# A block step with attention and 16,384 experts: the products of the first 96 expert tiles taken as one of 512 columns and one of 256, and the halves of a bank added afterwards

## What is computed

```
q = (h @ w_q).reshape(C, PEER_HEADS, 2, D_KEY // 2)
s = jnp.einsum('cphd,phkd->cphk', q, sub_keys)
s1, i1 = lax.top_k(s[:, :, 0], PEER_TOPK); s2, i2 = lax.top_k(s[:, :, 1], PEER_TOPK)
cand = s1[..., :, None] + s2[..., None, :]; cidx = i1 * N_KEYS + i2   # all pairs
top_s, top_i = lax.top_k(cand, PEER_TOPK);  e = cidx at top_i;  g = softmax(top_s)
a = jax.nn.gelu(jnp.einsum('cpkd,cd->cpk', u_tab[e], h))
f = jnp.einsum('cpk,cpkd->cd', g * a, v_tab[e])
```

## Time and profile before

| | |
|---|---|
| median of 3 runs | 1099.77 us (1098.5 to 1102.85) |
| the profiled execution | 1107.55 us, of which its span is 1105.9 us |
| busy share of the span | PE 96%, PEld 86%, DVE 77%, ACT 50%, POOL 12% |
| 512 KB loads and 128 KB stores of the up tiles | 128 each |

### The profile page before, as it was taken

The page is one execution under the profiler, slowest core; times in us unless marked ns, Lnnn a source line. Parts: engine busy times, 40 slices in busy tenths (PEclk is TensorE's granted clock), DMA queues, the critical chain, the costliest instruction groups (busy, mean ns, idle before and its releaser), DMA issues.

```text
span 1105.9 us, 23553 instructions
## 1 busy us (share of the span) xinstructions
PE 1066.5 (96%) x7256; PEld 954.3 (86%) x7256; DVE 856.9 (77%) x1950; ACT 555.2 (50%) x1057; POOL 137.8 (12%) x153
## 2 busy tenths in 40 slices
PE   6999989889999999999999999999999999999996
PEld 6997645879999999999999999998788888888875
DVE  4324353788988888887658999978888888888877
ACT  4435454544453544443554555545555555555543
POOL 0244401100001000454100000001010101010100
PEclk9999986989999999999999999999999999999998
DMA  7655903243458866899974444458888888888872
GB/s 252 259 204 185 350 39 115 84 145 115 139 186 276 272 236 230 310 409 392 319 249 140 139 140 143 142 165 276 319 284 296 281 294 286 296 286 289 293 236 90
DMA packets 96248, 253.19 MB, mean 229 GB/s; under 512 B 11424, under 2 KB 44224, under 8 KB 95408
## 3 DMA queue, kind: packets, MB, share of 16 engines
q1 hardware_dynamic: 81840, 196.84, 51.5%
q0 software_dynamic: 14368, 55.87, 14.4%
HBM read 232.60 MB, written 22.12 MB: 230 GB/s over the span
## 4 chain that ended last, share of the span: by engine, by line
PE 85%; DMA 7%; DVE 4%; ACT 2%; issue 1%; SPq 0%; DVEq 0%; ACTq 0%
PE ps L541 13%; PE ps L542 13%; PE ps L543 12%; PE ps L993 10%; PE ps L995 10%; PE ps L994 10%; DMA activations<-u_out 6%; PE ps L966 5%; PE ps L625 1%; DVE w_lo L1358 1%; PE ps L897 1%; PE ps L772 1%; DMA a_in<-activations 1%; PE ps L980 1%; PE ps L769 0%
## 5 line engine op out<-in xcount | busy, mean ns | idle before, releaser
L1358 DVE TENSOR_TENSOR w_lo<-ring,w_hi 128x512 fp32r<-128x512 f32 (+1 forms) x458 | 389.5, 853 | 137.7 <-ACT w_hi L1041 124.1
L1041 ACT CAST w_hi<-ring 128x512 fp32r<-128x512 f32 (+1 forms) x460 | 345.8, 752 | 98.7 <-PE ps L995 62.5
L541 PE MATMUL ps<-h_hi,w_hi 128*128 128x256 f32 (+1 forms) x1128 | 330.6, 293 | 3.0 <-DVE w_lo L1358 3.0
L542 PE MATMUL ps<-h_lo,w_hi 128*128 128x256 f32 (+1 forms) x1128 | 321.0, 285 | 0.0
L543 PE MATMUL ps<-h_hi,w_lo 128*128 128x256 f32 (+1 forms) x1128 | 319.3, 283 | 0.0
L541 PEld LDWEIGHTS ps<-h_hi,w_hi 128*128 128x128 f32 x1128 | 214.9, 191 | 7.0 <-issue 3.9
L542 PEld LDWEIGHTS ps<-h_lo,w_hi 128*128 128x128 f32 x1128 | 214.2, 190 | 0.0
L543 PEld LDWEIGHTS ps<-h_hi,w_lo 128*128 128x128 f32 x1128 | 211.8, 188 | 0.0
L993 PE MATMUL ps<-w_hi,y_hi 128*128 128x512 f32 x512 | 199.8, 390 | 0.7 <-DVE y_lo L1823 0.5
L994 PE MATMUL ps<-w_hi,y_lo 128*128 128x512 f32 x512 | 199.2, 389 | 0.0
L995 PE MATMUL ps<-w_lo,y_hi 128*128 128x512 f32 x512 | 199.2, 389 | 0.0
(11 more groups left out here) (349 smaller groups left out, 1274.9 us busy)
## 6 DMA issues: line engine op xcount, KB each, us to landing
ring<-in_uT_dram SPq DMA_DIRECT2D x128, 512.0 KB, 3.6
ring<-in_v_dram SPq DMA_DIRECT2D x128, 512.0 KB, 4.4
activations<-u_out SPq DMA_DIRECT2D x128, 128.0 KB, 3.3
a_in<-activations SPq DMA_DIRECT2D x128, 128.0 KB, 4.2
ring<-in_w_in_dram SPq DMA_DIRECT2D x22, 512.0 KB, 4.4
ring<-in_w_q_dram SPq DMA_DIRECT2D x16, 512.0 KB, 3.2
ks<-in_cache_sb_dram POOLq DMA_DIRECT2D x16, 256.0 KB, 3.2
vs<-in_cache_sb_dram POOLq DMA_DIRECT2D x16, 256.0 KB, 5.4
```

What stands on the lines that cost most here:

```text
L541: mm(out, hi, hi_, start=start, stop=False)
L542: mm(out, hi, lo_, start=False, stop=False)
L1041: nc.scalar.copy(w_hi[slot][:, x], ring[:, ring_slot, x]).then_inc(part_hi, 2 if half is None else 1)
L1358: V.tensor_tensor(w_lo[slot][:, x], ring[:, ring_slot, x], w_hi[slot][:, x].bitcast(F32), ALU.subtract).then_inc(part_lo[ring_slot], 2 if ...
```

## The change

The two copies of `h` are placed as one tile `h_both` with a fixed distance between the low and the high half, so that one matmul can stream 256 low columns and 256 high columns. For the first 96 up tiles, `up_tile` issues for each block of rows one product of `w_hi` with 512 columns (low half of the bank: `w_hi*h_lo`; high half: `w_hi*h_hi`) and one of `w_lo` with `h_hi`, 256 columns, into the high half: 16 matmuls instead of 24. The two halves must then be added. ACT copies the low half to `u_sum` (four buffers), DVE adds the high half to it (`halves_added`), and ACT takes gelu from there.

The order on ACT changes with it: `up_step` of tile t issues `high` of tile t + 4 first, then the copy of tile t, then gelu of tile t - 1. DVE adds the halves of tile t directly behind `low` of tile t + 4. PE waits for the addition of tile t - 4 before it writes that bank again. `PACE` goes from 1.2 to 1.05. `u_sum` lies where `w_lo` of the gate stage's second slot lies, so DVE waits for gelu of the last tiles before it goes on to the gates. SP's program, the 32 up tiles of the gate stage, and the down tiles are not changed.

```diff
-PACE, PACE_Q = 1.2, 2.0
+PACE, PACE_Q = 1.05, 2.0
...
+        h_apart = at_h - (at_con + NLIVE)
+        h_both = at("h_both", [128, 2, h_apart], at_con + NLIVE, F32R)
...
+        u_sum = at("u_sum", [128, 4, DT], at_w1 + 3 * D)
...
+            def up_tile(slot, bank, lows):
+                both = ps[:, bank, :].rearrange("p (a t) -> p a t", a=2)
+                for kd in range(KD):
+                    if kd % 4 == 0:
+                        pe.wait_ge(lows[0], lows[1 + kd // 4])
+                    block_ = slice(kd * 128, (kd + 1) * 128)
+                    last = kd == KD - 1
+                    if last:
+                        mm(both[:, 1, :], w_lo[slot][:, block_], h_hi[:, kd, 0:DT], start=False, stop=False)
+                    ins = mm(both, w_hi[slot][:, block_], h_both[:, :, kd * T:kd * T + DT], start=kd == 0, stop=last)
+                    if not last:
+                        ins = mm(both[:, 1, :], w_lo[slot][:, block_], h_hi[:, kd, 0:DT], start=False, stop=False)
+                    if kd % 4 == 3:
+                        ins.then_inc(w_mm, 1)
...
-                        pe.wait_ge(u_act, 4 * i + r + 1)
-                        project((AT_U + r) % 4, h_parts, r, halves(i, AT_U + r), width=DT)
+                        pe.wait_ge(u_add, 4 * i + r + 1)
+                        up_tile((AT_U + r) % 4, r, halves(i, AT_U + r))
...
-            def gelu_then_high(i, r, first=0):
-
-                gelu(i, r, first)
-                n = AT_U + first + r + 4
-                slot, value = filled(n)
-                high(slot, 16 * i + value, place(n))
+                t = first + r
+                if first < U_ALONE:
+                    act.wait_ge(u_add, 4 * i + (4 + t + 1))
+                else:
+                    act.wait_ge(w_mm, 8 * i + 2 * (AT_U + t + 1))
+                if t >= 2:
+                    act.wait_ge(spill[t % 2], 32 * i + 16 * (t // 2))
+                x = u_sum[:, t % 4, :] if first < U_ALONE else ps[:, r, 0:DT]
+                A(u_out[:, t % 2, :], x, ACT.Gelu_apprx_tanh).then_inc(u_act, 1)
+
+            def up_step(i, r, first=0, next_high=True):
+
+                n = AT_U + first + r
+                if next_high:
+                    slot, value = filled(n + 4)
+                    high(slot, 16 * i + value, place(n + 4), used=8 * i + 2 * (n + 1))
+                else:
+                    act.wait_ge(w_mm, 8 * i + 2 * (n + 1))
+                nc.scalar.copy(u_sum[:, r % 4, :], ps[:, r % 4, 0:DT]).then_inc(u_low, 1)
+                if first + r >= 1:
+                    gelu(i, r - 1, first)
...
+            def halves_added(m):
+                dve.wait_ge(u_low, m + 1)
+                V.tensor_tensor(u_sum[:, m % 4, :], u_sum[:, m % 4, :], ps[:, m % 4, DT:2 * DT], ALU.add).then_inc(u_add, 1)
...
                 lows[0] = n + 1
+                if n >= AT_U + 4:
+                    halves_added(n - AT_U - 4)
...
+            halves_added(U_ALONE - 4)
             low_half(0, m0, 0)
             low_half(0, m0, 1)
+            halves_added(U_ALONE - 3)
+            dve.wait_ge(u_act, 4 + U_ALONE - 2)
             low_half(0, m0 + 1, 0)
+            halves_added(U_ALONE - 2)
+            halves_added(U_ALONE - 1)
+            dve.wait_ge(u_act, 4 + U_ALONE)
```

More of the change, by code:

```diff
@@ L246, in trunk @@
         os_ = at("os_", [128, 2, 128], at_w1 + 1536)
-        h_hi = at("h_hi", [128, KD, T], at_h, F32R)
-        h_lo = at("h_lo", [128, KD, T], at_con + NLIVE, F32R)
+        h_apart = at_h - (at_con + NLIVE)
+        h_both = at("h_both", [128, 2, h_apart], at_con + NLIVE, F32R)
+        h_lo, h_hi = [h_both[:, q, 0:KD * T].rearrange("p (c t) -> p c t", t=T) for q in range(2)]
         E = [at_e + 2 * D * q for q in range(4)]
@@ L349, in trunk @@
         rt_exp_in, rt_exp, rt_pick, rt_t, rt_slot = map(sem, ("rt_exp_in", "rt_exp", "rt_pick", "rt_t", "rt_slot"))
-        u_act, one_ready, g_mm, g_sb = map(sem, ("u_act", "one_ready", "g_mm", "g_sb"))
+        u_act, u_low, u_add, one_ready, g_mm, g_sb = map(sem, ("u_act", "u_low", "u_add", "one_ready", "g_mm", "g_sb"))
         spill = [sem(f"spill{r}") for r in range(2)]
@@ L926, in _ @@
                 pe.wait_ge(q_sb, 4 + 12 + r + 1)
-                pe.wait_ge(u_act, r + 1)
-                project((AT_U + r) % 4, h_parts, r, halves(0, AT_U + r), width=DT)
+                up_tile((AT_U + r) % 4, r, halves(0, AT_U + r))
             pe.wait_ge(h4_ready, 1)
@@ L1269, in _ @@
                     scores_out(14 + r)
-                gelu_then_high(0, r)
+                up_step(0, r)
             act.wait_ge(hr_mm, 1)
@@ L1274, in _ @@
                 for r in range(4):
-                    gelu_then_high(i, r, 4)
+                    up_step(i, r, 4)
             act.wait_ge(rt_exp_in, 3)
@@ L1287, in _ @@
                     A(sact[:, :], sact[:, :], ACT.Gelu_apprx_tanh).then_inc(s_act, 1)
[L1288 to L1291, removed]
+                up_step(0, r, U_ALONE - 8, next_high=r < 6)
+            gelu(0, 3, U_ALONE - 4)
             with act.Fori(0, DT // 32) as i:
@@ L1359, in low @@
                                 ALU.subtract).then_inc(part_lo[ring_slot], 2 if half is None else 1)
+            def halves_added(m):
+                dve.wait_ge(u_low, m + 1)
+                V.tensor_tensor(u_sum[:, m % 4, :], u_sum[:, m % 4, :], ps[:, m % 4, DT:2 * DT], ALU.add).then_inc(u_add, 1)
+            dve.sem_inc(u_add, 4)
             lows, routed = [0], []
```

## The result

The changed kernel takes 1155.74 us in the median (1146.52 to 1157.54, 5 runs); the kernel before took 1102.13 us beside it (1098.5 to 1103.95, 5 runs). The ratio is 1.047, with a 95% interval of 1.0437 to 1.0502. The forecast of 1119 us had the direction and missed the size; the time lies above the range. The profiled execution of the changed kernel took 1146.52 us, its span 1144.8 us. It is the shortest of the five. Its 96 up tiles begin at 298.4 us, not at 304.1 as in the trace before, and the stages ahead of them are not touched by the change.

A forecast was written before the change was run, and what follows sets the result against it. PE was taken to bound the quiet up tiles, the gelu-store chain with full DMA engines those with gathers. +3.6 + 13.0 + 2.7 = +19.3 us on 1099.77 gives 1119 us; the range takes in 1101 and ends at 1141.

The forecast's parts named there:

- The mechanism: In the 96 up tiles, gelu moved behind a later cast closes a loop of waits over ACT and SP.
- the ring: Up tiles: gelu, store, load, landing, cast, copy, gelu; two tiles a turn, 2.40 us plus the landing.
- the passage: From the last up tiles to the gates: PE waits for the last copy, addition, gelu and first pair; +2.7 us (0 to +4).
- the landing: Up tiles: time for a weight tile's load to arrive; 3.4 us in the quiet part, 4.6 us with gathers.
- PE's shorter tile: Up tiles on PE: 2.76 us a tile instead of 2.85, 8.4 us in all, not collected and in no term.
- quiet tiles: The 65.5 up tiles without dot products: 2.90 us a tile against 2.85, +3.6 us (-5.9 to +14).
- tiles with gathers: The 30.5 up tiles with dot products, while rows are gathered: 3.50 us a tile, +13.0 us (-5.3 to +48).
- rival 3: Up tiles: the gather keeps the DMA engines full, landing 6.9 us, +48 there; 1154 us in all, chance 0.06.
- Rival 1: Up tiles: the ring does not bind, 2.92 us a tile with gathers; sum -7.9, 1092 us, chance 0.08.

The follow-up runs named there:

- experiment 3: Kernel before, with only ACT's order changed: cast of tile t + 4 first, then gelu of tile t - 1; 1133.83 us, ratio 1.0282.
- experiment 6: Changed kernel with SP's store one tile later only while the 96 tiles are loaded, `u_sum` left in place; 1106.72 us, ratio 1.0023.
- experiment 5: Changed kernel with SP's store one tile later only while the 96 tiles are loaded, and `u_sum` moved; 1099.74 us, ratio 0.996.
- experiment 4: Changed kernel with `u_sum` at a free address and the last two additions behind `scaled_id`; 1146.94 us, ratio 1.0401.
- experiment 7: Changed kernel with POOL gathering only the first four row blocks, the other 28 left out; 1141.01 us, ratio 1.0339.

## Why the prediction was right in kind and wrong in size

**The mechanism** was right: experiment 3 makes most of the loss, and experiment 6 takes it back, by the order of waits alone. The chain runs through load, cast, copy, gelu and store; the casts wait for landings 71 times; the DMA share falls below 1. All of these were named as signs.

**What failed** is the size of the ring's turn and of the passage. The turn was forecast at 5.80 us without gathers and 7.00 with them, and is 6.08 and 7.60, the landing being the term that missed most (4.6 us forecast with gathers, 5.09 measured up to the cast). The first four gathers stood in no term and cost 5.1 us. And the passage, +2.7 us, left out that the last gelus wait for landings of stores and that PE waits for a gelu as well: it cost 8.0.

**PE's shorter tile.** Forecast 2.76 us; where PE doesn't wait it is 2.78. The timeline of PE in experiment 5, one tile apart:

```profile
399.79 0.28 PE L939 MATMUL ps<-h_both,w_lo 128*128 128x256 f32 x1
399.91 0.39 PE L937 MATMUL ps<-h_both,w_hi 128*128 128x512 f32 x1
400.14 0.28 PE L939 MATMUL ps<-h_both,w_lo 128*128 128x256 f32 x1
...
402.58 0.28 PE L939 MATMUL ps<-h_both,w_lo 128*128 128x256 f32 x1
```

A block of rows takes 2.783/8 = 347.9 ns against 356.4 before, so an instruction saved is worth 8.5 ns, not 10.9. The rule that the Trainium skill states (TensorE: Matmul & The Clock Gate, "Wait — 56ns, not 53.3ns?"), 2.5 ns a matmul, is further off than the rows of the down tiles were. Of this only 1.1 us was collected, in the first 16 tiles; the forecast was nothing.

**DVE.** Forecast 0.35 to 0.42 us for an addition, measured 0.415. From 325 to 450 us of the changed kernel, grouped by form:

```profile
L1387 DVE TENSOR_TENSOR u_sum<-u_sum,ps 128x256 f32<-128x256 f32 x40 | 16.6, 415 | 0.0
```

**The terms of the ring.** Means over all turns, worked out from the rows of ACT and SP (us):

| | forecast quiet | measured | forecast gathers | measured |
|---|---|---|---|---|
| gelu to store's issue | 0.56 | 0.61 | 0.56 | 0.61 |
| store to load | 0.60 | 0.70 | 0.60 | 0.69 |
| load to cast (landing) | 3.4 | 3.68 | 4.6 | 5.09 |
| cast to gelu | 1.24 | 1.32 | 1.24 | 1.22 |
| turn | 5.80 | 6.31 | 7.00 | 7.60 |

All terms but one were too small, and in a closed ring such misses add up. The quiet turn was to be 0.10 us above two old tiles of 2.85. Its measured column holds the turns that the first four gathers slowed too. Behind them, from tile 24 to 60, a tile takes 3.04 us, a turn 6.08; the loads of tiles 30 to 55 have 0.61, 0.68, 3.52 and 1.25 us in the four rows. Two of the reasons are plain. The store-to-load time was read from one pair of rows, but once in four it is 0.97 us, where SP's loop begins anew (487.42 to 488.39 above). And between the landing and the cast lie 0.15 us (492.90 to 493.06) that the sum didn't have. The landings up to 9.3 us are not the spread of a quiet stretch: in the kernel before they are loads issued from 351 to 355 us, when POOL had just issued its first four gathers, and there they cost nothing, since PE stays at 2.85 us a tile.

**The sum.** Forecast +19.3, trace +44.9. The 25.6 us of difference are:

- quiet tiles: +3.6 forecast. Measured -1.1 to tile 16, +6.8 from 24 to 60 (3.04 us a tile), +5.0 from 89 to g0: +10.7, so 7.1 too few. (The +3.6 also takes 0.055 us a tile where its own numbers, 2.90 less 2.85, give 0.05, so +3.3.)
- the first four gathers, which POOL issues at once at 352 us. They lie in the part that I took for quiet and were in no term: +5.1.
- tiles with gathers: +13.0 forecast, +21.1 measured. The landing, up to the cast, settled at 5.09 us at 318 GB/s. I had taken 4.6, nearer to the row at 277 GB/s; the straight line between the two rows was the better choice. The prediction has it settle at 3.7 us a tile; worked out again it settles at 3.8 us and some 315 GB/s, +22, and 3.73 was measured. The same tiles of the kernel before took 3.00 us each, not the 93.8/30.5 = 3.08 of the forecast.
- the passage: +2.7 forecast, +8.0 measured.

**The passage** missed two waits. The timelines of ACT and of DVE there:

```profile
619.04 0.42 ACT L1279 ACTIVATE u_out<-u_sum 128x256 f32<-128x256 f32 x1 [1.24 <-DMA activations<-u_out]
621.65 0.42 ACT L1279 ACTIVATE u_out<-u_sum 128x256 f32<-128x256 f32 x1 [2.19 <-DMA activations<-u_out]
```

```profile
618.19 0.74 DVE L1387 TENSOR_TENSOR u_sum<-u_sum,ps 128x256 f32<-128x256 f32 x2
622.10 0.23 DVE L1838 TENSOR_SCALAR scaled_id<-con 128x128 f32<-128x128 f32 x1 [3.17 <-ACT u_out L1279]
...
623.36 0.42 DVE L1849 TENSOR_TENSOR one_b<-con,slotT 128x256 f32<-128x256 f32 x1
```

I counted copy, addition, gelu and the pair, but not that the last two gelus, now close together, each wait for the landing of the store of two tiles earlier (1.24 and 2.19 us), and not that PE waits for a gelu before the first tile of the gate stage. PE stands 5.5 us for `one_b` and 1.9 before it for that gelu. Together that is 7.4 of the 8.0 us; the lower clock behind it can account for the rest, which was not tried apart.

**Range and chances.** The range ended at 1141, +41 us; the trace alone, at +44.9, is above it, and the median, at +53.6, more so; 8.7 us of that are in no trace. Its ends left out what the forecast left out, the first gathers and the two gelus that wait for stores. The time of rival 3, 1154, is close to the result for a wrong reason: it asked for a landing of 6.9 us and DMA engines kept full, and they were at 0.92. Rival 1's tile of 2.92 us with gathers is about what the opened ring gives (2.94 in experiment 5, 2.81 in 6).

## What to carry to other kernels

Before an operation is moved behind another in an engine's queue, follow its result round through every in-order queue back to itself, and count how many tiles one turn moves: the change halved that number, from four to two. Such a ring is to be priced with mean durations, the loop's own branch, the hand-over from a landing to the engine and the slowest stretch included, since nothing in it can be made up later. And a product that is made cheaper on PE is worth its price only if the loads don't hang on its result: here one store moved by one tile in SP's queue was worth some 49 us to the changed kernel (ratio 1.040 in experiment 4, 0.996 in experiment 5), for a net gain over the kernel before of 0.4% (0.1 to 0.7%).

## What the runs showed of the hardware

- A slower ring unloads the DMA engines and so partly pays for itself: with gathers, loads of 512 KB took 5.1 us up to the cast (0.15 us of it hand-over) at 318 GB/s, and their landings took 6.9 at 386 in the kernel before. At the low end the volume does not decide: in experiment 7, at 210 GB/s, the chain shows landings of 3.7 to 3.8 us, no shorter than the median of 3.4 at 244 before. Why is open.
- PE's clock fell around short stands. PE waited 1.9 us up to 617.1 us and 5.5 us up to 623.9 us. The granted clock was 0.74 from 615 to 620 us, 0.50 from 620 to 625 (the 1.2 GHz level), 0.73 from 625 to 630, and 1.00 from 630. In experiment 5, with a stand of 1.2 us, it stayed at 1.00. It also fell among the tiles with gathers, where PE's waits just before were 1.8 and 1.9 us: 0.66 from 510 to 515 us and 0.73 from 540 to 545. There the low level lasted 6.8 us in all, so it can have cost at most some 3.4 of the 21.1 us.
